# Pooled chains at fixed steps between the gates' products, type sums dealt out over the order units, and later places for x rows and vectors, in a hybrid decoder step on 8 cores

## What is computed

```
h  = rmsnorm(x, g_pre_mix);  p = h @ w_in      # [xv | B | C | u | gate_conv | gate_pool], 1024 columns each
ya = (B * causal_dwconv3(C * xv)) @ w_out_conv
yb = pool_scale * groupwise(trailing_mean_w(u) - u)     # w = 2, 4, 8, 16 in four groups of 256 channels
merged = sigmoid(gate_conv + b) * ya + sigmoid(gate_pool + b) * yb
x  = x + rmsnorm(merged @ w_o, g_post_mix)
f  = square(relu(rmsnorm(x, g_pre_mlp) @ w_up)) @ w_down      # width 4096
x  = x + rmsnorm(f, g_post_mlp)
```

## Time and profile before

| | before |
|---|---|
| median of 3 executions | 947.56 us (946.59 to 948.27) |
| the profiled execution | 946.2 us |
| span of its slowest core (7) | 944.9 us |
| spans of the eight cores | 931.8 to 944.9 us |
| TensorE busy, share of the span | 96% |
| VectorE | 70% |
| ScalarE | 43% |
| GpSimd | 13% |

### The profile page before, as it was taken

The page is one execution under the profiler, slowest core; times in us unless marked ns, Lnnn a source line. Parts: engine busy times, 40 slices in busy tenths (PEclk is TensorE's granted clock), DMA queues, the critical chain, the costliest instruction groups (busy, mean ns, idle before and its releaser), DMA issues.

```text
span 944.9 us, 15572 instructions; the slowest of 8 cores (931.8 to 944.9 us)
## 1 busy us (share of the span) xinstructions
PE 907.1 (96%) x5015; PEld 442.0 (47%) x5015; DVE 664.3 (70%) x988; ACT 406.7 (43%) x830; POOL 123.2 (13%) x170
## 2 busy tenths in 40 slices
PE   7999999979999999999999999996999999999997
PEld 5744444434545454544454444442444555544443
DVE  3677787786677775786998988548577675546187
ACT  3534454423344446435345777410224566620213
POOL 6300000000122120000000010000040111110022
PEclk9999999999999999999999999997999999999999
DMA  9999648868466764524766899990495366095036
GB/s 196 241 237 162 110 102 170 164 149 172 92 135 165 149 159 83 115 74 108 214 147 224 123 150 158 119 189 19 109 226 159 65 103 121 2 160 108 1 109 247
DMA packets 61374, 130.73 MB, mean 138 GB/s; under 512 B 31600, under 2 KB 31856, under 8 KB 60016
## 3 DMA queue, kind: packets, MB, share of 16 engines
q0 software_dynamic: 19872, 73.41, 44.0%
q1 hardware_dynamic: 41136, 56.05, 21.6%
q10 hardware_dynamic: 288, 0.30, 0.1%
HBM read 165.25 MB, written 23.20 MB: 199 GB/s over the span
## 4 chain that ended last, share of the span: by engine, by line
PE 78%; DVE 9%; DMA 6%; issue 4%; ACT 1%; POOL 1%; DVEq 0%; ACTq 0%; POOLq 0%
PE PS L139 78%; DVE AR L159 4%; DMA AR<-w_dn 4%; DVE AR L169 3%; DMA AR<-x_p 2%; DVE AR L809 1%; ACT AR L156 1%; POOL AR L129 1%; DVEq L224 0%; PE PS L143 0%; DVE FAC L507 0%; DVE FAC L164 0%; DVE STAT L429 0%; ACT ZO L156 0%; DVE CS L164 0%
## 5 line engine op out<-in xcount | busy, mean ns | idle before, releaser
L139 PE MATMUL PS<-AR 128*128 128x512 bf16 (+1 forms) x4928 | 896.0, 344 | 27.9 <-DVE AR L159 21.7
L139 PEld LDWEIGHTS PS<-AR 128*128 128x128 bf16 x4928 | 435.8, 98 | 486.9 <-issue 41.6
L156 ACT ACTIVATE AR<-PS 128x512 f32<-128x512 f32 (+3 forms) x314 | 184.9, 600 | 287.2 <-PE PS L139 259.8
L159 DVE TENSOR_TENSOR AR<-PS,AR 128x512 f32<-128x512 f32 (+3 forms) x297 | 189.8, 655 | 122.4 <-PE PS L139 111.0
L159 DVE TENSOR_TENSOR AR<-AR 128x1024 bf16<-128x1024 bf16 (+9 forms) x237 | 203.4, 885 | 66.1 <-PE PS L139 29.8
L156 ACT ACTIVATE AR<-AR 128x512 bf16<-128x512 f32 (+4 forms) x179 | 116.7, 671 | 73.9 <-DVE AR L159 51.1
L156 ACT ACTIVATE AR<-AR,CS 128x512 f32<-128x512 f32 (+1 forms) x88 | 58.1, 688 | 138.9 <-DVE AR L159 138.5
L169 DVE SCALAR_TENSOR_TENSOR AR<-AR,CS 128x512 f32<-128x512 f32 (+1 forms) x80 | 65.3, 816 | 35.5 <-ACT AR L156 17.4
L159 POOL TENSOR_TENSOR AR<-AR 128x1024 f32<-128x1024 f32 (+1 forms) x25 | 48.5, 1939 | 300.7 <-DVE AR L169 117.4
L169 DVE SCALAR_TENSOR_TENSOR AR<-AR,STAT 128x1024 bf16<-128x1024 f32 (+2 forms) x51 | 60.6, 1201 | 6.1 <-DVE STAT L1083 1.3
L169 DVE SCALAR_TENSOR_TENSOR AR<-AR 128x512 bf16<-128x512 f32 (+4 forms) x100 | 60.5, 631 | 4.3 <-DVE AR L809 0.5
(11 more groups left out here) (40 smaller groups left out, 89.3 us busy)
## 6 DMA issues: line engine op xcount, KB each, us to landing
AR<-w_dn POOLq DMA_DIRECT2D x32, 512.0 KB, 18.0
AR<-w_m POOLq DMA_DIRECT2D x16, 768.0 KB, 11.0
AR<-w_up POOLq DMA_DIRECT2D x16, 768.0 KB, 7.7
AR<-x_p SPq DMA_DIRECT2D x18, 512.0 KB, 4.5
x_d<-AR SPq DMA_DIRECT2D x17, 512.0 KB, 3.9
AR<-x_d SPq DMA_DIRECT2D x17, 512.0 KB, 7.7
AR<-x_p POOLq DMA_DIRECT2D x14, 512.0 KB, 19.5
AR<-w_a POOLq DMA_DIRECT2D x24, 256.0 KB, 20.6
```

Of the source, the lines that this page charges most:

```text
L139: return self.add("pe", lambda e: e.matmul(out, lhsT, rhs, start=start, stop=stop, **kw), reads=[lhsT, rhs], writes=[out], signal=sig, nam ...
L156: return self.add("act", lambda e: e.activation(out, in_, func, **kw), reads=rd, writes=wr, name=name)
L159: return self.add(eng, lambda e: e.tensor_tensor(out, in0, in1, op), reads=[in0, in1], writes=[out], name=name)
```

## The change

Four edits. First, the chains of blocks 2 to 7 for the two large groups leave steps 3 to 6. A table `CHAIN_AT` gives each a place: chain (j, e) (e = 0 for ta, 1 for tb) runs at (2,0): step (0,2), between the gates' additions and the next products; (2,1): behind step (0,5); (3,0): behind (0,6); (3,1): behind the u step of block 4, tb; (4,0): behind the u step of block 5, ta; (4,1): behind (1,1); (5,0): inside (1,2); (5,1): behind (1,5); (6,0) and (6,1): behind the u steps of blocks 6 and 7, tb; (7,0): behind (2,1); (7,1): inside (2,2). The sample's chains stay in step 6. Second, half 0's type sums 0 and 2 swap their buffers, and their four pieces run behind order units 0, 2 (type sum 0), 4 and 9 (type sum 2) where they had been behind 5, 6 and 2, 3. Third, `b0_vectors` stands behind step (3,4) where it had been behind (3,1). Fourth, for half 0 GPO and x1 rows 0 to 2 are written in `d2` where they had been in `d0`.

```diff
+        CHAIN_AT = {(0, 2): (2, 0), (0, 5): (2, 1), (0, 6): (3, 0), ("u", 4, 1): (3, 1), ("u", 5, 0): (4, 0),
+                    (1, 1): (4, 1), (1, 2): (5, 0), (1, 5): (5, 1), ("u", 6, 1): (6, 0), ("u", 7, 1): (6, 1), (2, 1): (7, 0), (2, 2): (7, 1)}
...
-        GT = [[(117504, 121600), (146176, 150272), (152320, 113408), (87296, 89344)],
+        GT = [[(152320, 113408), (146176, 150272), (117504, 121600), (87296, 89344)],
...
+        def pooled_at(h, at):
+
+            if at in CHAIN_AT:
+                j, e = CHAIN_AT[at]
+                u_chain.pop((h, j, HTG[h][e]))()
+
...
-            def pooled(e, tg):
-                if g < 3:
-                    u_chain.pop((h, 2 * g + 2 + e, tg))()
+            def pooled(at):
+                pooled_at(h, at)
...
+                pooled((g, 2))
...
-                pooled(0, ta)
...
-                pooled(0, tb)
...
-                pooled(1, ta)
...
-                pooled(1, tb)
                 if h == 1:
                     for e, m in enumerate(ms):
                         m_smp(m)
-                        pooled(e, 4)
+                        if g < 3:
+                            u_chain.pop((h, 2 * g + 2 + e, 4))()
...
                 u_chain[(h, j, tg)] = u_unit(j, tg)
+                if tg in tgs[:2]:
+                    pooled_at(h, ("u", j, tgs.index(tg)))
...
-                    add((g, n_ + 1), own + (nxt if n_ == 4 else []), fn)
+                    add((g, n_ + 1), own + (nxt if n_ == 4 else []),
+                        lambda fn=fn, at=(g, n_ + 1): (fn(), at[1] != 2 and pooled_at(h, at)))
...
-        after(ph[0][(3, 1)], b0_vectors)
+        after(ph[0][(3, 4)], b0_vectors)
...
-        for n_, i, p in ((2, 2, 0), (3, 2, 1), (5, 0, 0), (6, 0, 1)):
+        for n_, i, p in ((0, 0, 0), (2, 0, 1), (4, 2, 0), (9, 2, 1)):
...
-            if half == 0:
-                P.dma("sp", GPO, bcast(g_post_mlp), "gpo")
-            load_xl(*((0, 1, 2) if half == 0 else (SMP, 8)))
+            if half == 1:
+                load_xl(SMP, 8)
...
             if half == 1:
                 dn["sr"] = grab()
+            else:
+                P.dma("sp", GPO, bcast(g_post_mlp), "gpo")
+                load_xl(0, 1, 2)
```

## The result

The changed kernel took 934.89 us (the profiled execution) and 933.07, beside 947.08 for the kernel before (median of 4, 946.39 to 948.27). The ratio is 0.986 (95% interval 0.9835 to 0.9886): 1.4% faster. In other executions of any of these kernels, the ones before and after alike, the cores of a die ran at a lower granted clock for tens of us more; they are in no number here. The forecast was 933.5.

The account below looks back on a forecast made before the run. TensorE, busy 907.1 of 944.9 us, was taken as the bound, only idle or slow-clock time winnable. Gains of 14.4 (core 7) and 12.7 (core 0) left the slowest core at 930.9, 14.0 less, so 933.5 on the median; range 925 to 940.

Parts of the forecast that it names:

- Order units: Three short TensorE waits for VectorE, 1.39 together, shrink by one type-sum piece, 0.59, to 0.80.
- Round 0: Half 0, phase B: at step 4 a wait of 0.3 stays; 1.4 won, order units included.
- Round 1: Half 0, phase B: four chains beside u steps, then chain (5,0) of 2.34; wait at step 4 is 0, at most 0.3.
- Round 2 and half 1: Phase B: round 2's merges come about 4 us earlier and its stalls go; half 1's waits go but for up to 0.3.
- 0.77, 2.86, 1.69 of clock: Half 0: waits of 0.77 and 2.86 around round 3's start, and 1.69 of half clock after them, all go.
- 5.60: Half 1, phase B: TensorE waits in rounds 0 to 2 and at round 3's start sum to 5.60; up to 0.3 stays.
- the clock term: Half clock near 200 us costs core 7 1.69; core 0 had no drop, its gain without this is 12.7.
- x rows and vectors: Residual's x rows go about 14 us later, with 28 of 41.7 us of slack left: cost 0, bounds 0 and 3.
- GPO and x1 rows: Down steps, half 0: SyncE goes by its waits, so the later step changes nothing; booked 0, bounds 0 and the whole w_dn stall.
- rival 1: The fourth edit works or the w_dn stall melts otherwise: 922.8, half of it 928; chance 0.11.
- Cores 7 and 0 keep a stall of 9 to 10: Half 0's down steps: VectorE's waits for w_dn pieces, 9.88 and 9.30 before, stay on these two cores.
- the signs that the prediction itself named: No TensorE idle over 0.4 from 115 to 450 us, no half clock near 200, w_dn stall unchanged, GPO still issued early.

Follow-up runs that it names:

- e2_types_vectors: Kernel before with only the change's type sums, their buffers and b0_vectors place (edits 2 and 3): ratio 1.0008.
- e11_best: Changed kernel with tile 16's transpose behind step (2,2), GPO and x1 rows held until d1's last matmul, chain (5,0) behind step (1,4): ratio 0.9802.
- e12_no_fourth: Changed kernel with only its fourth edit undone, GPO and x1 rows 0 to 2 written in d0 again: ratio 0.9895.
- e7_late16: Changed kernel with the DMA transpose of tile 16 moved from step (1,5) to (2,2): ratio 0.9859.
- e8_late16_held: Changed kernel with tile 16's transpose moved to (2,2) and GPO and x1 rows held until the last matmul of d1: ratio 0.9769.
- e4_plain_all: Changed kernel with every DMA transpose replaced by a plain DMA of the same bytes, for timing only: ratio 0.9742, 922.5 us.
- e1: Kernel before with only the change's first edit, the chains at their new steps: ratio 0.9897.
- e3: Changed kernel with GPO and the x1 rows behind it held until the last matmul of d1: ratio 0.9871.

## Why the prediction was right, and where it was not

**Order units.** Forecast 0.80 left, measured 0.18 + 0.18 + 0.28 = 0.64. The waits shrank by 0.75 where one piece (0.59) was booked; that fits one piece fewer ahead of them, with 0.16 left over. By themselves these edits bring nothing that can be measured (`e2_types_vectors`).

**Round 0.** Forecast 0.3 left, measured 0.17, and that one has no releaser but issue.

**Round 1.** Forecast 0 to 0.3, measured 0.58 on all eight cores. The step that failed is the walk through VectorE's order from the u steps to step 3. VectorE of core 1:

```profile
155.31 1.28 DVE L159 TENSOR_TENSOR AR<-PS,AR 128x512 f32<-128x512 f32 x2
156.51 1.25 DVE L809 TENSOR_TENSOR_SCAN AR<-AR 128x527 f32<-128x527 f32 x1
157.86 0.69 DVE L169 SCALAR_TENSOR_TENSOR AR<-AR 128x512 bf16<-128x512 f32 x1
158.47 0.16 DVE L159 TENSOR_TENSOR AR<-AR,FAC 128x7 f32<-128x7 f32 x1
159.09 0.17 DVE L169 SCALAR_TENSOR_TENSOR AR<-AR 128x7 bf16<-128x7 f32 x1 [0.46 <-DVE AR L159]
159.26 1.89 DVE L159 TENSOR_TENSOR AR<-PS,AR 128x512 f32<-128x512 f32 x3
```

Chain (5,0) lasts from 156.51 to 159.26, 2.75 in place of 2.34: its last short instruction waits 0.46 for the one ahead of it. The four chains in a row end at 155.31, having begun at 146.47: 8.84 in place of 8.3 to 8.6. These 0.4 and 0.2 to 0.5 are the difference. Restart is 0.84 behind the additions' start, close to the 0.94 that was used. `e11_best` shows that this chain is the one.

**Round 2 and half 1.** The forecast was that 0.77, 2.86, 1.69 of clock and nearly all of 5.60 go. Core 0's unbroken run to 480.3 shows all of them gone. The fastest core lost 15.7. It is core 1 before, and there the clock hadn't dropped:

```profile
209.37 167.20 PE L139 MATMUL PS<-AR 128*128 128x512 bf16 x940 [2.86 <-ACT AR L156]
```

So its forecast is the one without the clock term, 12.7. TensorE's idle times from the order units on add to 14.4 us on it and to 1.4 on core 7 after, 13.0 less: this is what the forecast was about, and it was right. Of the other 2.7 about 1.0 is an earlier start of the order units, where the change does nothing (cores before differ by 2 us there), and 1.5 is less matmul time, with a mean clock of 0.998 after 0.996; neither was tested.

**x rows and vectors.** Forecast 0, measured 0: no wait stands near 245 us, and `e2_types_vectors` is at 1.0008.

**GPO and x1 rows.** Forecast 0 for the edit, since SyncE goes by its waits. Right: in the changed kernel core 7 issues GPO at 578.42 and core 1 at 595.88, while TensorE is in the up steps, and `e12_no_fourth` is within the scatter. The price put on rival 1, a real hold, was 10.7 us (933.5 to 922.8). The runs give 0.7% or 6.7 us on the kernel before, and from `e7_late16` to `e8_late16_held` 0.9859 - 0.9769 = 0.9% or 8.5 us: right in kind, somewhat too high. The prediction held that such a hold would end the stall; it shortens it.

**Cores 7 and 0 keep a stall of 9 to 10.** This step failed. The stall isn't tied to a core: it was on 7, 0, 2 and, which the prediction left out, 5 (3.21) before, on 5 after, on 1, 3, 4 and 7 in `e7_late16`. Nor are the long spans: core 1 of the changed kernel had 933.5 us in the profiled execution and 916.0 in the next on the same chip. The sum took it as a property of the cores that it was seen on; it comes and goes from one execution to the next, and the slowest of eight cores mostly has one. Since its size was kept in the sum, this alone would have left the time right.

**The new stall.** No rival named it. The walk through phase B priced each wait on engines and no load on the way: it asked when VectorE would make the weight sums, not whether `w_m` would be there, nor which DMA the earlier sums would release on SyncE ahead of it. The end of core 1 is set by this (11.45 and 0.48, and 2.8 of clock), and it happens to be about as long as the `w_dn` stall with its clock. The forecast of 933.5 so hit the time by a mechanism that was right for the gain, and by luck for the rest, which was right in size and wrong in place and cause. By the signs that the prediction itself named it failed in three: the stall left cores 7 and 0, a wait over 0.4 sits at step 4 of round 1, and on core 1 the granted clock is 0.68 from 210 to 220 us. Without both stalls the same edits reach 922.5 (`e4_plain_all`); with the one gone and the other shortened 924.3 (`e8_late16_held`, median).

**Still open.** Why the transpose is late on some cores and not on others, at equal order and distance. Whether it is the transposes' own path or an interplay of cores: in the changed kernel, `e1`, `e3` and `e12` no core had both a long `w_m` and a long `w_dn` wait, which would fit a crowd that a late core misses, but nothing tested it. And the waits of 1 to 2 us near 840.

## What to carry to other kernels

When VectorE work is moved out of a step, list what the step's earlier end releases, on the DMA queues too: a store that comes early can let the transfer behind it pass a load that is needed sooner. Put the load that is needed soon ahead of a transpose, or the transpose in another step. Writing a transfer into a later step delays it only if something there makes it wait; a queue that has run ahead needs a dependency. And before a stall is booked to a core, look whether it stays there in a second execution; the time is the worst of eight, so two chance stalls have to be cured together before either cure shows.

## What was not expected of the hardware

DMA transposes can jam the DMA engines of a core. From 180 to 190 us the transposes' packets took 0.50 us each on core 1 and 0.017 on core 0, for the same instructions issued in the same order; a load of 768 KB landed after 38.9 us in place of 10.9. The Trainium skill (DMA: Bandwidth & Descriptors, Rules for kernel authors) says that a transpose next to ordinary DMAs "needs nothing". That stands in a row on what must be ordered for the data to be right; for time, the runs show that it does need something. Issued within 1.3 us of the load, the transpose itself landed after more than 20 us on 30 of 72 cores, in the kernel before too; the load was late with it on 14 of the 40 where the transpose went 1.0 us ahead, and on none of the 24 where it came 1.3 us behind. Replacing the transposes by plain copies of the same bytes brought the changed kernel from 0.986 to 0.9742 of the kernel before, with both stalls gone.
